# Padding of 16 and 8 bytes per K tile in the activations of the two down projections

## What is computed

```python
# first layer
h2 = rms_norm(x, norm_mlp_g)
x = x + jnp.square(jax.nn.relu(h2 @ w_mlp_up)) @ w_mlp_down        # 1024 -> 4096 -> 1024
...
# second layer
hn = rmsnorm(h, g_ffn)
h = h + (jax.nn.silu(hn @ w_gate) * (hn @ w_up)) @ w_down          # 1024 -> 2816 -> 1024
```

## Time and profile before

| | |
|---|---|
| median of 3 runs | 901.51 us (901.18 to 901.99) |
| profiled execution, its own time | 902.32 us |
| its span | 900.5 us |
| TensorE busy (matmuls) | 889.2 us, 99% |
| TensorE weight loads busy | 764.4 us, 85% |
| VectorE busy | 587.0 us, 65% |
| ScalarE busy | 447.9 us, 50% |
| GpSimd busy | 113.0 us, 13% |
| granted TensorE clock | 1.0 (2.4 GHz) |

### The profile page before, as it was taken

The page is one execution under the profiler, slowest core; times in us unless marked ns, Lnnn a source line. Parts: engine busy times, 40 slices in busy tenths (PEclk is TensorE's granted clock), DMA queues, the critical chain, the costliest instruction groups (busy, mean ns, idle before and its releaser), DMA issues.

```text
span 900.5 us, 12630 instructions
## 1 busy us (share of the span) xinstructions
PE 889.2 (99%) x5035; PEld 764.4 (85%) x5035; DVE 587.0 (65%) x850; ACT 447.9 (50%) x631; POOL 113.0 (13%) x84
## 2 busy tenths in 40 slices
PE   9999999999999999999999999999999999999998
PEld 6887787888978999988888889888888888888886
DVE  5478978997787566645355747977785565555542
ACT  6265456854535555543345335646554544444531
POOL 0431225665110000000000002100100000000200
PEclk9999999999999999999999999999999999999999
DMA  8874542344225555566568635533542565554562
GB/s 289 203 250 142 186 140 69 126 142 120 95 95 187 158 181 182 182 193 201 199 194 282 203 102 193 170 111 104 178 139 91 166 200 183 186 179 136 196 230 70
DMA packets 83554, 149.74 MB, mean 166 GB/s; under 512 B 8480, under 2 KB 16208, under 8 KB 83376
## 3 DMA queue, kind: packets, MB, share of 16 engines
q1 hardware_dynamic: 80352, 144.55, 49.4%
q10 hardware_dynamic: 2528, 3.63, 1.1%
q0 software_dynamic: 624, 0.87, 0.8%
HBM read 147.59 MB, written 1.44 MB: 166 GB/s over the span
## 4 chain that ended last, share of the span: by engine, by line
PE 87%; DVE 7%; DMA 3%; ACT 1%; issue 1%; POOL 0%; SPq 0%; DVEq 0%; ACTq 0%; POOLq 0%
PE gemm L497 64%; PE mixbank L991 5%; PE gemm L991 5%; DMA raw<-in_w_in_dram 2%; DVE w_lo L1823 2%; PE mixbank L560 1%; PE mixbank L657 1%; PE mixbank L682 1%; DMA x<-in_x_dram 1%; PE mixbank L852 1%; PE mixbank L1163 1%; DVE mix L1944 1%; PE gemm L1191 1%; PE mixbank L668 1%; ACT w_hi L1270 1%
## 5 line engine op out<-in xcount | busy, mean ns | idle before, releaser
L1823 DVE TENSOR_TENSOR w_lo<-raw,w_hi 128x2048 fp32r<-128x2048 f32 (+3 forms) x131 | 284.8, 2184 | 186.0 <-ACT w_hi L1270 185.9
L1270 ACT ACTIVATE w_hi<-raw 128x2048 fp32r<-128x2048 f32 (+3 forms) x140 | 255.4, 1833 | 173.7 <-DMA raw<-in_w_in_dram 52.0
L497 PE MATMUL gemm<-w_hi,s_hi 128*128 128x512 f32 (+3 forms) x784 | 209.2, 387 | 1.0 <-issue 0.5
L497 PE MATMUL gemm<-w_lo,s_hi 128*128 128x512 f32 (+3 forms) x784 | 201.9, 377 | 1.2 <-DVE w_lo L1823 1.1
L497 PE MATMUL gemm<-w_hi,s_lo 128*128 128x512 f32 (+3 forms) x784 | 201.7, 377 | 0.0
L497 PEld LDWEIGHTS gemm<-w_lo,s_hi 128*128 128x128 f32 x784 | 142.6, 188 | 29.1 <-DVE w_lo L1823 1.9
L497 PEld LDWEIGHTS gemm<-w_hi,s_lo 128*128 128x128 f32 x784 | 142.7, 188 | 27.6
L497 PEld LDWEIGHTS gemm<-w_hi,s_hi 128*128 128x128 f32 x784 | 139.6, 188 | 27.4 <-issue 2.5
L2636 POOL TENSOR_TENSOR sm<-sm 128x2 f32<-128x2 f32 (+5 forms) x13 | 22.0, 1695 | 458.2 <-DVE sm L1867 300.9
L2630 POOL TENSOR_TENSOR w_lo<-raw,w_hi 128x2048 fp32r<-128x2048 f32 x9 | 41.3, 4606 | 157.4 <-ACT w_hi L1270 157.4
L1287 ACT ACTIVATE mix<-gemm,sm 128x512 f32<-128x512 f32 (+2 forms) x25 | 16.3, 653 | 53.7 <-PE gemm L497 53.7
(11 more groups left out here) (352 smaller groups left out, 1163.7 us busy)
## 6 DMA issues: line engine op xcount, KB each, us to landing
raw<-in_w_in_dram SPq DMA_DIRECT2D x40, 1024.0 KB, 5.1
raw<-in_w_mlp_up_dram SPq DMA_DIRECT2D x16, 1024.0 KB, 5.6
raw<-in_w_mlp_down_dram SPq DMA_DIRECT2D x16, 1024.0 KB, 5.1
raw<-in_w_gate_dram SPq DMA_DIRECT2D x10, 1024.0 KB, 5.1
raw<-in_w_up_dram SPq DMA_DIRECT2D x10, 1024.0 KB, 5.1
raw<-in_w_down_dram SPq DMA_DIRECT2D x10, 1024.0 KB, 5.1
raw<-in_w_out_dram SPq DMA_DIRECT2D x8, 1024.0 KB, 5.2
raw<-in_w_xkv_dram SPq DMA_DIRECT2D x8, 1024.0 KB, 5.1
```

Source lines behind the costliest of these rows:

```text
L497: return nc.tensor.matmul(G[b % 2][t][:, 0:width], lhs, rhs, start=kt == 0 and not (low_x or low_w), stop=kt == blk["kt"] - 1 and (low_x i ...
L1270: nc.scalar.activation(w_hi[:, n % SLOTS, 0:kn, 0:width], raw[:, n % SLOTS, 0:kn, 0:width], ACT.Copy)\
L1823: V.tensor_tensor(w_lo[:, s, 0:kn, 0:width], raw[:, s, 0:kn, 0:width], w_hi[:, s, 0:kn, 0:width].bitcast(F32), ALU.subtract)\
```

## The change

Each K tile of `hT_hi` and `hT_lo` takes 260 float32 values per partition instead of 256 (16 bytes more), each K tile of `h2_hi` and `h2_lo` 258 (8 bytes more). The names then stand for views of the first 256 values of each tile; everything that reads or writes them is written as before. What lies behind these tensors in the same region (`hid`; `hid2`, `sg2`) moves up by 1024 bytes and by 352 bytes.

```diff
-        hT_hi = sb("hT_hi", [P, DFF // P, SEQ], F32R, a2)
-        hT_lo = sb("hT_lo", [P, DFF // P, SEQ], F32R, a2)
+        hT_hi = sb("hT_hi", [P, DFF // P, SEQ + 4], F32R, a2)[:, :, 0:SEQ]
+        hT_lo = sb("hT_lo", [P, DFF // P, SEQ + 4], F32R, a2)[:, :, 0:SEQ]
         hid = sb("hid", [P, 2, 4, SEQ], F32, a2)
...
-        h2_hi = sb("h2_hi", [P, DFF2 // P, SEQ], F32R, a4)
-        h2_lo = sb("h2_lo", [P, DFF2 // P, SEQ], F32R, a4)
+        h2_hi = sb("h2_hi", [P, DFF2 // P, SEQ + 2], F32R, a4)[:, :, 0:SEQ]
+        h2_lo = sb("h2_lo", [P, DFF2 // P, SEQ + 2], F32R, a4)[:, :, 0:SEQ]
         hid2 = sb("hid2", [P, NT, NCOL], F32, a4)
         sg2 = sb("sg2", [P, 2, NT, NCOL], F32, a4)
```

## The result

The changed kernel takes 904.68 us (median of 6 runs, 904.45 to 905.93), the kernel before 901.59 us (901.18 to 901.99). The ratio is 1.0038, with a 95% interval of 1.0025 to 1.0050: 3.1 us lost, outside the range of the prediction. Its profiled execution has a span of 902.9 us and a time of 904.73.

A forecast was written before the change was run, and what follows sets the result against it. TensorE's matmul distance was taken as the bound. The profiled 902.32 us plus 0 for each down projection's loads and 0 for the writers gave 902.3, or 901.5 us for a median; range 900.3 to 902.9.

The forecast's parts named there:

- Reading the bound: Whole span: TensorE busy 99% at 2.4 GHz, so matmul distance, 226.8 and 227.0 ns, sets both down projections' time.
- The writers, what moves up behind the padding, waits: VectorE and ScalarE writes in two runs of 256, and shifted `hid`, `hid2`, `sg2`: 0 us, with at least 20 us of cover.
- Addresses of the loads ... I take 0: Stationary loads at shifted K tiles, 384 in the first down projection and 264 in the second: 0 change taken for each.
- leftover of 13.4 ns: Part of each 226.8 ns matmul distance beyond streaming 512 columns at one per cycle, 213.4 ns; said not to depend on addresses.
- four pairs of tensors with two K steps: Operand pairs of both down projections, a block on `s_hi`/`s_lo` and the first up projection, claimed to share the same leftover.
- The second argument: Within a pair of K tiles, most load steps stay between `t` = 0 and 1 of one tile, unchanged by padding.
- The price of a misaligned load: Second down projection, 132 loads off 16 bytes: taken as 0, since a load must grow over 39 ns to delay a matmul.
- The slower one: Rival: misaligned loads at odd K tiles of the second down projection set the pace, 1.7 or 19.7 us lost; chance 0.05.
- The faster rival: Both down projections: padding removes a conflict between tiles at equal low address bits, up to 8.7 us gained; chance 0.03.

## Why the prediction was wrong

**Reading the bound: right.** TensorE's matmul distance in the two projections sets their time, and the whole difference sits there.

**The writers, what moves up behind the padding, waits: right.** L2313, L2592 and L1594 last what they lasted, to 2 ns, and no wait appeared. The padding of 256 and 512 bytes, with the same form of writers, is free. In the second layer the built program moves `hid2` and `sg2` up by 384 bytes and not by 352, because tensor sizes are rounded up there, and `h2_lo` by 192; so K tile kt of `h2_lo` begins 192 + 8 kt bytes further on, not 8 kt.

**The step that failed: "Addresses of the loads ... I take 0", in both projections.** Its argument was that the leftover of 13.4 ns is the same for four pairs of tensors with two K steps. That is true, but the four pairs were one case, not four: all of them have both operands at the same place modulo 256 bytes. The rows could show that a step of 1024 or 2048 makes no difference; they held nothing on an offset between moving and stationary operand. The second argument was misread too: of the twelve steps from one load to the next in a pair, only half stay within one K tile, not most. Measured: 5.2 ns on each of 384 matmuls and 5.4 ns on each of 240, in place of 0. The padding breaks two conditions at once, the equal place modulo 256 and the multiple of 32. The first alone is enough for a price of this size: padding of 32 bytes costs 5.7 ns a matmul (232.5).

**The price of a misaligned load: wrong mechanism.** I counted a weight load as free until it grew by 39 ns, and found the nearest row for its growth in L1105. No load grew: 188 ns in the changed kernel as before. The matmul distance grew by 5 ns with 39 ns of apparent room. Nor was it the misalignment of the load: a shift of the weights, which leaves the stationary operand of L497 where it was, costs 4.8 ns in the first down projection, and 64 and 128 bytes on the stationary operand cost 6.5 and 5.6 ns beside 6.5 for 16. L1105 was no witness: its products move 128 columns and not 512, and the products with 256 columns show that what holds for 512 need not hold for fewer.

**The rivals.** The slower one had its sign right and its place half right: it gave the whole loss to odd K tiles of the second projection, where the first, with its 16 bytes, lost more (2.00 us against 1.30). Its prices were 1.7 and 19.7 us, and the measured 3.1 lies between, because neither was the price of what happens. The sentence "the leftover has the same size" had also closed the case of a small price per matmul everywhere; 648 matmuls make 3 us out of 5 ns, and a range that allowed the leftover of 13.4 ns to change in either direction, up to 8.7 us, would have held the result. The faster rival, a conflict at equal low address bits, is the wrong way round: equal bits are the good case here.

**The rule of the Trainium skill on 16 byte lines** (SBUF — State Buffer, the box on SBUF cachelines) pointed to a loss for the 8 bytes, but does not say what the runs show: by it 128 bytes would be free and 16 as well, and both cost over 5 ns. The Trainium skill (same page, Who interferes with whom) also has TensorE's read ports wait for no other engine, which is not contradicted, since both operands here are TensorE's own; but its table calls the two ports independent, and the prediction took from it that there is no conflict for a skew to remove, or to make. Here the distance depends on how the operands of the two ports lie to each other (226.8 ns, or 232.4 with one of them 128 bytes further on), and the measurement decides. What happens at the ports themselves no run shows.

**What stays open.** Shown is what the distance of matmuls of 512 columns depends on: the place of the moving and the stationary operand relative to each other modulo 256 bytes, and for both a multiple of 32 bytes (one run, with 16 bytes, shows the second). The first rests on shifts of the activations against the weights; no run shifted the weights alone by a multiple of 32, and how the price of 16 bytes divides between the two conditions is not known. That the streaming of one matmul and the load of the next meet in the same part of the memory would fit, and also that equal places let them run without meeting; the even 226 and 227 ns in the one case and long repeating cycles in the other look like two processes that fall into step or do not. Against it, with the activations a constant 16 bytes further on the distances are slow and yet even (232 to 235 ns). None of this was shown by itself, and it does not explain why 256 columns go faster with the weights 16 bytes off, with equal places or not.

## What to carry to other kernels

Rows that agree are evidence only for what differs between them: look up where the tensors lie before you conclude from several pairs that addresses don't matter. If operands of float32 matmuls of 512 columns are padded or shifted, keep the moving and the stationary one at the same place modulo 256 bytes, and at multiples of 32; padding of 256 bytes per tile was free, 8 to 128 cost about 2% of each such matmul. With fewer columns measure anew: at 256 the shift that costs at 512 gained 1.3%. When TensorE is busy 99% of the span, a few ns per instruction are the scale on which a change must be costed.

## What the runs showed of the hardware that I had not expected

- The distance of 512 column matmuls is 226.8 ns with both operands at the same place modulo 256 bytes; with the stationary one off by 8, 16, 64 and 128 bytes it is 230.8, 233.3, 233.4 and 232.4 ns, with weight loads still recorded at 187 to 192 ns.
- Shifting moving and stationary operand together by 32, 64 or 128 bytes costs nothing; together by 16 bytes it is 230.0 to 233.3 ns, 231.1 in the first down projection.
- Matmuls with 256 moving columns (L991) go the other way: 118.4 ns with the stationary weights off by 16 bytes, whether the moving activations are off as well or not, 120.0 with both where they were or both shifted by 32, 64 or 128 bytes. The kernel that uses it takes 0.9989 of the time of the one before (0.9980 to 0.9998).
- The distances repeat: in the changed kernel's first down projection to 1 ns over K tiles with the same padding modulo 256 and over both blocks, but for the first few matmuls and the last pair.
